# The expert layer's weighted sum on 64x64 quarters of the TensorE array, two gathered rows at a time

## The chip, the cores and the metric

The kernel runs on one core of a Trainium2 chip. The metric is the device time of one execution in microseconds (us), lower is better. A core has five engines with an instruction queue each: TensorE (PE, matmuls, its weight loads shown apart as PEld), VectorE (DVE), ScalarE (ACT), GpSimd (POOL) and SyncE (SP), and 16 DMA engines that move data. Engines wait for each other by semaphores.

## The reference

Two transformer blocks on 512 tokens of width 1024, in float32. The part that matters here is the expert layer of the first block. Each token picks, in each of 8 heads, its 16 best of 16384 experts, so 128 experts a token; an expert is a row u (1024 numbers) and a row v (1024 numbers) of a table. The output is the sum of the v rows, each weighted by gelu(u . x) times its gate:

```python
def one_block(xb):                                   # 128 tokens
    ...
    top_s, pos = lax.top_k(cand_s, PEER_TOPK)
    experts = jnp.take_along_axis(cand_i, pos, axis=-1).reshape(PEER_BLOCK, PEER_HEADS * PEER_TOPK)
    gates = jax.nn.softmax(top_s, axis=-1).reshape(PEER_BLOCK, PEER_HEADS * PEER_TOPK)
    u = u_table[experts]
    hid = jax.nn.gelu(jnp.einsum('nkd,nd->nk', u, xb).astype(jnp.float32), approximate=False) * gates
    return jnp.einsum('nk,nkd->nd', hid.astype(xb.dtype), v_table[experts])
```

## The kernel before

`build` runs the stages one after the other. The one that changes is `peer_experts`. It works on 4 tiles of 128 tokens (`TT`), one token on each of the 128 partitions. A tile has 128 **slots**: slot n is the n-th chosen expert of every token. The slots of one head, 16 of them, are called a **unit** here; there are 32 units. The device loop `Fori(0, PAIRS)` does two units in each round.

What happens to a slot, in order:

1. POOL (L1209) issues one indirect DMA that gathers, for each of the 128 tokens, one row of 8 KB (u and v side by side) into one of the 8 buffers of `rows` (`RING` = 8). Ahead of it POOL waits for `slot_free`, which says that the buffer's former slot has been summed, and once a unit for `routed`, the experts' numbers.
2. DVE (L1286) waits for the landing and forms the dot product of u with the token (`hid`, semaphore `dotted`).
3. ACT takes the gelu (L1330), the product with the gate (L1331), and then writes `diag` (L1333): the 128x128 identity with each row scaled by the token's weight.
4. PE (L1359) waits for `diag_ready` and multiplies `diag` by the v half of the buffer, in two matmuls of 512 columns, which add into `peer_y` in PSUM. Each float32 matmul runs as two passes over the array, so the trace has four MATMUL records a slot. The last one raises `slot_free`.

Between two units DVE does `route`: a long chain of small instructions that finds the 16 experts and gates of the next unit. It begins with a wait for `gates_free`, which ACT raises when it has done all 16 slots of the unit before, and the dots of the next unit stand behind it in DVE's queue. POOL's gathers run up to 8 slots ahead of PE, so the routes are made one unit ahead of the dots: the route of unit u+1 stands ahead of the dots of unit u.

`zero` (L1346) opens and closes each tile's sum with matmuls of zeros. `add_tile` (L1292) adds a tile's sum to `t.x` on DVE; for tile 0 it stands at the end of the loop of tile 1, and so on; those of tiles 2 and 3 both stand at the very end. The order on each engine is the order in which the code is written; there is no scheduler.

Two other lines serve as a comparison. `first_attention` has matmuls with only 64 rows of the array (L571 and L572): two of its products, `score0` and `score1`, use the rows 0 to 63 and 64 to 127. In `scores` they are written as all of half 0, then all of half 1:

```python
for half in range(2):
    rows = slice(half * AHD, (half + 1) * AHD)
    q = t.fm[rows, h, NM + i * P:NM + (i + 1) * P]
    pe.matmul(score[half][:, BANK - NM:BANK], q, t.fm[rows, AH + h, 0:NM], start=True, stop=True)
    pe.matmul(score[half][:, BANK:BANK + (i + 1) * P], q, t.fm[rows, AH + h, NM:NM + (i + 1) * P], ...)
```

Of the kernel before, what the change touches and what calls it, by code (L numbers as in the profile page):

```python
# [18 lines left out]
ALU = mybir.AluOpType  # L19
ACT = mybir.ActivationFunctionType  # L20
AX = mybir.AxisListType

P = 128
D = 1024
KC = D // P
T = 512
TT = T // P
# [3 lines left out]
BANK = 512  # L31
# [10 lines left out]
SLOTS = PH * TOPK  # L42
# [70 lines left out]
def sbuf(nc, ctx, name, shape, dtype=F32):  # L113
    return ctx.enter_context(nc.sbuf_tensor(numbered(name), shape, dtype))


def psum(nc, ctx, name, shape):
    return ctx.enter_context(nc.psum_tensor(numbered(name), shape, F32))
# [1035 lines left out]
def peer_experts(core, t, dram, hidden, scores):  # L1154
# [3 lines left out]
    nc = core.nc  # L1158
    RING, PAIRS = 8, PH // 2
    PER = 2 * TOPK  # L1160
    with ExitStack() as ctx:
        rows = sbuf(nc, ctx, "rows", [P, RING, 2 * D])
        hid = sbuf(nc, ctx, "hid", [P, 3, RING])
        diag = sbuf(nc, ctx, "diag", [P, RING, P])
        zeros = sbuf(nc, ctx, "zeros", [P, BANK])
        step16 = sbuf(nc, ctx, "step16", [P, TOPK])

# [13 lines left out]
        experts = sbuf(nc, ctx, "experts", [P, 2, TOPK], U32)  # L1181
        gates = sbuf(nc, ctx, "gates", [P, 2, TOPK])
        soft = sbuf(nc, ctx, "soft", [P, 3, TOPK])
        y = [psum(nc, ctx, f"peer_y{i}", [P, D]) for i in range(2)]
        step_in, ready, go = core.sem("step16_in"), core.sem("zeros_ready"), core.sem("gather_go")
        got = [core.sem(f"rows_in{i}") for i in range(RING)]
        routed, logits, exped, gates_free = [core.sem(f"peer_{n}") for n in ("routed", "logits", "exped", "gates_free")]
        dotted, diag_ready, slot_free, summed, added = [
            core.sem(f"peer_{n}") for n in ("dotted", "diag_ready", "slot_free", "summed", "added")]
        search_go = core.sem("search_go")  # L1190
        block = ctx.enter_context(nc.Block())

# [21 lines left out]
        def _(dve):  # L1214
            chain = core.chain(dve, "dve_step")
            dve.memset(zeros[:, :], 0.0).then_inc(ready, 1)
            dve.wait_ge(step_in, 16)
            start = chain.count
            per_route = ROUTE_LINKS
# [69 lines left out]

            def add_tile(tile):  # L1290
                dve.wait_ge(summed, tile + 1)
                dve.tensor_tensor(t.x[:, tile, :], t.x[:, tile, :], y[tile % 2][:, :], ALU.add).then_inc(added, 1)  # L1292

            route(0, 0)
            assert chain.count - start == per_route, (chain.count - start)
# [12 lines left out]
        @block.scalar  # L1308
        def _(act):
            chain = core.chain(act, "act_step")  # L1310

            act.sem_inc(gates_free, 1)

            def exponentials(unit):
                act.wait_ge(logits, unit + 1)
                act.activation(soft[:, 1, :], soft[:, 0, :], ACT.Exp).then_inc(exped, 1)

            exponentials(0)
            for tile in range(TT):
                with act.Fori(0, PAIRS) as j:  # L1320
                    chain.base = j * (2 * PER)
                    for p in range(2):

                        act.sem_inc(gates_free, 1)
                        exponentials(tile * PH + j * 2 + (p + 1))
                        for k in range(TOPK):
                            n = p * TOPK + k
                            b = n % RING
                            act.wait_ge(dotted, tile * SLOTS + j * PER + (n + 1))
                            chain.link(act.activation(hid[:, 1, b:b + 1], hid[:, 0, b:b + 1], ACT.Gelu))  # L1330
                            chain.link(act.activation(hid[:, 2, b:b + 1], hid[:, 1, b:b + 1], ACT.Copy,  # L1331
                                                      scale=gates[:, p, k:k + 1]))
                            act.activation(diag[:, b, :], t.ident[:, :], ACT.Copy, scale=hid[:, 2, b:b + 1])\  # L1333
                               .then_inc(diag_ready, 1)
                chain.base = 0
                chain.count += (PAIRS - 1) * 2 * PER

        @block.tensor
        def _(pe):
            pe.sem_inc(slot_free, RING)  # L1340
            pe.wait_ge(ready, 1)

            def zero(tile, start):

                for c in range(2):
                    last = pe.matmul(y[tile % 2][:, c * BANK:(c + 1) * BANK], t.ident[:, :], zeros[:, :],  # L1346
                                     start=start, stop=not start)
                return last

            for tile in range(TT):  # L1350
                if tile >= 2:
                    pe.wait_ge(added, tile - 1)
                zero(tile, True)
                with pe.Fori(0, PAIRS) as j:
                    for n in range(PER):
                        b = n % RING
                        pe.wait_ge(diag_ready, tile * SLOTS + j * PER + (n + 1))
                        for c in range(2):
                            last = pe.matmul(y[tile % 2][:, c * BANK:(c + 1) * BANK], diag[:, b, :],  # L1359
                                             rows[:, b, D + c * BANK:D + (c + 1) * BANK], start=False, stop=False)  # L1360
                        last.then_inc(slot_free, 1)
                zero(tile, False).then_inc(summed, 1)


# [1053 lines left out]
```

## Time and profile before

| | |
|---|---|
| time, median of 3 runs | 3526.93 us (3525.37 to 3530.85) |
| time of the profiled execution | 3526.79 us |
| its span | 3524.7 us |
| expert layer, first gather issued to last sum added | 700.6 to 2126.9 us of the span |
| busy in the span: PE, DVE, ACT, POOL | 78%, 52%, 32%, 19% |

The span is the time from the first to the last instruction in the profile; the execution's own time is 2.1 us longer. The rows below come from several views. The page has the busy share of each engine in 40 equal slices, the granted clock of TensorE (PEclk) and the DMA engines' share and rate. A table of stretches gives the same for stretches of our choice. The timeline has the instructions in order of time, equal neighbours merged, with the idle time of the engine before each in square brackets and who ended it. Busy shares tell how much an engine works; what a stage is bound by is read from who waits for whom.

### The profile page before, as it was taken

To read this page: it belongs to the slowest core of one execution; us is meant where nothing else is said; L and a number is where in the kernel's file an instruction comes from. 1 tells how busy PE (TensorE), PEld (TensorE's weight loads), DVE (VectorE), ACT (ScalarE), POOL (GpSimd) and SP (SyncE) were. 2 spreads that over 40 slices of the span, in tenths; PEclk is the share of its full clock that TensorE was granted. 3 is DMA by queue.
4 is the path that set the end of the run, shared out by engine and by line. 5 is a ranking of instruction groups with operands and counts; after the bars stand their busy time and mean duration, and the time that the engine had idled before them with its cause. 6 is when DMAs were issued, how large, how long until landed. Compare 5 with 4: busy or idle time off the path is not lost. (4 is left out here: it accounts for less than half of the span.)

```text
span 3524.7 us, 32413 instructions
## 1 busy us (share of the span) xinstructions
PE 2754.6 (78%) x10010; PEld 1784.0 (51%) x10010; DVE 1817.2 (52%) x3668; ACT 1123.1 (32%) x2491; POOL 671.8 (19%) x590
## 2 busy tenths in 40 slices
PE   5887778877677767767777676999889786979997
PEld 5864655622223222222232224887778434768875
DVE  5655743366666666666666664332363636243323
ACT  2212322233333333333333333222124235122211
POOL 1100000054444444444444440000000010000000
PEclk8995689988888888988888887999999688989998
DMA  5840012199999999999999992222132000222222
GB/s 181 295 155 1 1 48 78 45 400 381 377 382 377 379 368 381 382 376 381 380 376 379 374 377 94 96 96 72 60 97 62 1 33 1 96 80 100 84 84 78
DMA packets 118429, 705.60 MB, mean 200 GB/s; under 512 B 15184, under 2 KB 15840, under 8 KB 52128
## 3 DMA queue, kind: packets, MB, share of 16 engines
q0 software_dynamic: 81152, 576.40, 41.0%
q1 hardware_dynamic: 37168, 127.76, 10.5%
q8 instruction: 67, 1.10, 0.1%
q14 instruction: 42, 0.34, 0.0%
HBM read 702.01 MB, written 2.10 MB: 200 GB/s over the span
## 5 line engine op out<-in xcount | busy, mean ns | idle before, releaser
L1359 PE MATMUL peer_y<-rows,diag 128*128 128x512 f32 x2048 | 1001.5, 642 | 421.8 <-ACT diag L1333 421.2
L1359 PEld LDWEIGHTS peer_y<-rows,diag 128*128 128x128 f32 x2048 | 404.1, 205 | 1019.2 <-ACT diag L1333 599.7
L1286 DVE CUSTOM_DVE_ANT_0 rows<-rows,hidden 128x1024 f32<-128x1024 f32 x512 | 611.1, 1226 | 435.4 <-DMA rows<-in_peer_table,experts 429.5
L1209 POOL DMA_INDIRECT rows<-in_peer_table,experts x512 | 618.3, 1208 | 914.8 <-PE peer_y L1359 661.0
L1330 ACT ACTIVATE hid<-hid 128x1 f32<-128x1 f32 x512 | 103.9, 203 | 647.3 <-DVE hid L1286 647.2
L1333 ACT ACTIVATE diag<-ident,hid 128x128 f32<-128x128 f32 x512 | 205.5, 401 | 16.8
L1417 DVE TENSOR_TENSOR down_w_low<-down_raw,down_w_high 128x1024 fp32r<-128x1024 f32 x60 | 73.5, 1226 | 254.2 <-ACT down_w_high L1397 254.1
L399 ACT ACTIVATE proj_w_high<-proj_raw 128x1024 fp32r<-128x1024 f32 (+2 forms) x73 | 74.7, 1024 | 323.4 <-PE proj_bank L135 307.6
L426 DVE TENSOR_TENSOR proj_w_low<-proj_raw,proj_w_high 128x1024 fp32r<-128x1024 f32 (+2 forms) x73 | 85.9, 1178 | 147.4 <-ACT proj_w_high L399 145.7
L133 PE MATMUL g_bank<-ffn_feat_high,ffn_w_high 128*128 128x512 f32 x352 | 139.5, 396 | 27.7 <-DVE ffn_w_low L1504 27.7
L1504 DVE TENSOR_TENSOR ffn_w_low<-ffn_raw,ffn_w_high 128x2048 fp32r<-128x2048 f32 x44 | 100.9, 2292 | 115.1 <-ACT ffn_w_high L1486 115.1
L1331 ACT ACTIVATE hid<-hid,gates 128x1 f32<-128x1 f32 x512 | 150.9, 295 | 16.6
L133 PE MATMUL down_bank<-down_w_high,act_t_high 128*128 128x512 f32 x352 | 139.0, 395 | 16.5 <-DVE down_w_low L1417 16.5
L1512 DVE TENSOR_TENSOR silu<-silu,u_bank 128x512 f32<-128x512 f32 x44 | 30.3, 688 | 231.5 <-PE u_bank L135 231.5
L1397 ACT ACTIVATE down_w_high<-down_raw 128x1024 fp32r<-128x1024 f32 x60 | 63.6, 1060 | 262.6 <-PE down_bank L135 247.4
L134 PE MATMUL g_bank<-ffn_feat_low,ffn_w_high 128*128 128x512 f32 x352 | 138.8, 394 | 0.0
L135 PE MATMUL g_bank<-ffn_feat_high,ffn_w_low 128*128 128x512 f32 x352 | 138.7, 394 | 0.0
L134 PE MATMUL down_bank<-down_w_low,act_t_high 128*128 128x512 f32 x352 | 138.5, 393 | 0.0
L135 PE MATMUL down_bank<-down_w_high,act_t_low 128*128 128x512 f32 x352 | 138.3, 393 | 0.0
L133 PE MATMUL u_bank<-ffn_feat_high,ffn_w_high 128*128 128x512 f32 x352 | 137.0, 389 | 0.0
L135 PE MATMUL u_bank<-ffn_feat_high,ffn_w_low 128*128 128x512 f32 x352 | 137.0, 389 | 0.0
L134 PE MATMUL u_bank<-ffn_feat_low,ffn_w_high 128*128 128x512 f32 x352 | 137.0, 389 | 0.0
(420 smaller groups left out, 4558.5 us busy)
## 6 DMA issues: line engine op xcount, KB each, us to landing
ada<-in_w_ada POOLq DMA_DIRECT2D x48, 768.0 KB, 4.8
ffn_raw<-in_ffn_w_gate SPq DMA_DIRECT2D x44, 512.0 KB, 3.6
ffn_raw<-in_ffn_w_up SPq DMA_DIRECT2D x44, 512.0 KB, 4.5
down_raw<-in_ffn_w_down SPq DMA_DIRECT2D x44, 512.0 KB, 3.4
proj_raw<-in_w_in_f SPq DMA_DIRECT2D x16, 512.0 KB, 5.3
proj_raw<-in_peer_w_query SPq DMA_DIRECT2D x16, 512.0 KB, 3.3
rows<-in_peer_table,experts POOLq DMA_INDIRECT x512, 11.9
down_raw<-in_w_out SPq DMA_DIRECT2D x16, 512.0 KB, 3.5
```

Of the source, the lines that this page charges most:

```text
L133: pe.matmul(out, left[0], right[0], start=start, stop=False)
L134: pe.matmul(out, left[0], right[1], start=False, stop=False)
L135: return pe.matmul(out, left[1], right[0], start=False, stop=stop)
L399: act.activation(w.high[:, n % RING, 0:taken(slab)], w_raw[:, n % RAW, 0:taken(slab)], ACT.Copy)\
L426: dve.tensor_tensor(w.low[:, n % RING, 0:taken(slab)], w_raw[:, n % RAW, 0:taken(slab)], w.high[:, n % RING, 0:taken(slab)].bitcast(F32), ...
L1209: pool.indirect_dma_start(rows[:, n % RING, :], None, dram["peer_table"], bass.IndirectOffsetOnAxis(ap=experts[:, p, k:k + 1], axis=0))\
L1286: dve.tensor_tensor_reduce(out=rows[:, b, 0:D], in0=rows[:, b, 0:D], in1=hidden[:, tile, :], scale=1.0, scalar=0.0, op0=ALU.mult, op1=ALU.add,
L1330: chain.link(act.activation(hid[:, 1, b:b + 1], hid[:, 0, b:b + 1], ACT.Gelu))
L1331: chain.link(act.activation(hid[:, 2, b:b + 1], hid[:, 1, b:b + 1], ACT.Copy, scale=gates[:, p, k:k + 1]))
L1333: act.activation(diag[:, b, :], t.ident[:, :], ACT.Copy, scale=hid[:, 2, b:b + 1])\
L1359: last = pe.matmul(y[tile % 2][:, c * BANK:(c + 1) * BANK], diag[:, b, :], rows[:, b, D + c * BANK:D + (c + 1) * BANK], start=False, stop= ...
L1504: dve.tensor_tensor(w.low[:, f % 2, :, :], w_raw[:, f % 2, :, :], w.high[:, f % 2, :, :].bitcast(F32), ALU.subtract).then_inc(low.handle, 1)
```

## The change

A diagonal matrix has only zeros outside its diagonal blocks, so of the 128x128 array three quarters of a pass multiply nothing but the diagonal. The change keeps only two 64x64 blocks of each `diag`: block g holds the tokens of half g (partitions 0 to 63 or 64 to 127), and both stand side by side in a `diag` of 128x64. The array is used as four 64x64 quarters. A quarter is given by its rows (which half of the tokens comes in, g) and its columns (which half of the PSUM partitions goes out). Slot s of a pair uses the columns of half s. So even slots sum into partitions 0 to 63 and odd slots into 64 to 127, and each token half g has banks of its own: `peer_y00`, `peer_y01` for even tiles, `peer_y10`, `peer_y11` for odd ones (the last digit is g).

What this brings with it:

- PE waits for two diagonals, then issues 8 matmuls for two slots (before 2 for each slot), in the order (g, s) = (0,0), (1,1), (0,1), (1,0), for either 512 columns, and frees both buffers at the last one.
- ACT writes `diag` from `folded` (128x64) rather than from the identity (128x128). `folded` is made once by two copies on DVE.
- `zero` has 8 matmuls of 64x512 rather than 2 of 128x512.
- Half of each tile's sum lies on the other half's partitions. ACT's `cross` copies those two pieces into `crossed` at the end of a tile's loop, and `add_tile` now has two adds of 64x1024 from PSUM, and, once `cross_done` is there, one of 128x1024 with `crossed`.

```diff
-        diag = sbuf(nc, ctx, "diag", [P, RING, P])
+        folded = sbuf(nc, ctx, "folded", [P, HALVES])
+        diag = sbuf(nc, ctx, "diag", [P, RING, HALVES])
...
+            for own in GROUPS:
+                last = dve.tensor_copy(folded[own, :], t.ident[own, own])
+            last.then_inc(fold_done, 1)
...
             def add_tile(tile):
                 dve.wait_ge(summed, tile + 1)
-                dve.tensor_tensor(t.x[:, tile, :], t.x[:, tile, :], y[tile % 2][:, :], ALU.add).then_inc(added, 1)
+                for g, own in enumerate(GROUPS):
+                    last = dve.tensor_tensor(t.x[own, tile, :], t.x[own, tile, :], y[tile % 2][g][own, :], ALU.add)
+                last.then_inc(added, 1)
+                dve.wait_ge(added, 2 * tile + 1)
+                dve.wait_ge(cross_done, tile + 1)
+                dve.tensor_tensor(t.x[:, tile, :], t.x[:, tile, :], crossed[:, :], ALU.add).then_inc(added, 1)
...
+            def cross(tile):
+
+                act.wait_ge(summed, tile + 1)
+                if tile:
+                    act.wait_ge(added, 2 * tile)
+                for g, own in enumerate(GROUPS):
+                    last = act.activation(crossed[own, :], y[tile % 2][g][GROUPS[1 - g], :], ACT.Copy)
+                last.then_inc(cross_done, 1)
...
-                            act.activation(diag[:, b, :], t.ident[:, :], ACT.Copy, scale=hid[:, 2, b:b + 1])\
+                            act.activation(diag[:, b, :], folded[:, :], ACT.Copy, scale=hid[:, 2, b:b + 1])\
                                .then_inc(diag_ready, 1)
                 chain.base = 0
                 chain.count += (PAIRS - 1) * 2 * PER
+                if tile >= 1:
+                    cross(tile - 1)
+            cross(TT - 1)
...
-                    for n in range(PER):
-                        b = n % RING
-                        pe.wait_ge(diag_ready, tile * SLOTS + j * PER + (n + 1))
+                    for n in range(0, PER, 2):
+                        pe.wait_ge(diag_ready, tile * SLOTS + j * PER + (n + 2))
+                        pe.sem_inc(slot_go, 1)
                         for c in range(2):
-                            last = pe.matmul(y[tile % 2][:, c * BANK:(c + 1) * BANK], diag[:, b, :],
-                                             rows[:, b, D + c * BANK:D + (c + 1) * BANK], start=False, stop=False)
-                        last.then_inc(slot_free, 1)
+                            for g, s in ((0, 0), (1, 1), (0, 1), (1, 0)):
+                                b, rows_of = (n + s) % RING, GROUPS[g]
+                                last = pe.matmul(y[tile % 2][g][GROUPS[s], c * BANK:(c + 1) * BANK],
+                                                 diag[rows_of, b, :], rows[rows_of, b, D + c * BANK:D + (c + 1) * BANK],
+                                                 start=False, stop=False)
+                        last.then_inc(slot_free, 2)
```

How this stands in the engines' queues. First PE at the start of a tile's loop. Before, with a wait ahead of each slot's two matmuls:

```order
L1359 MATMUL peer_y0<-rows,diag 128x512 [waits peer_diag_ready]
L1359 MATMUL peer_y0<-rows,diag 128x512
L1357 REGISTER_ALU
L1359 MATMUL peer_y0<-rows,diag 128x512 [waits peer_diag_ready]
L1359 MATMUL peer_y0<-rows,diag 128x512
L1357 REGISTER_ALU
```

And in the changed kernel (`peer_y00` takes what comes in from tokens 0 to 63, `peer_y01` what comes from 64 to 127):

```order
L1390 MATMUL peer_y00<-rows,diag 64x512 [waits peer_diag_ready]
L1390 MATMUL peer_y01<-rows,diag 64x512
L1390 MATMUL peer_y00<-rows,diag 64x512
L1390 MATMUL peer_y01<-rows,diag 64x512
L1390 MATMUL peer_y00<-rows,diag 64x512
L1390 MATMUL peer_y01<-rows,diag 64x512
L1390 MATMUL peer_y00<-rows,diag 64x512
L1390 MATMUL peer_y01<-rows,diag 64x512
L1385 REGISTER_ALU
```

Eight matmuls now stand behind one wait where two stood, and neighbours alternate between the two row halves.

Second DVE at the very end of the layer, where the sums of tiles 2 and 3 are added. Before this is one row for both, and in the changed kernel:

```order
L1302 TENSOR_TENSOR x<-x,peer_y 64x1024 [waits peer_summed]
L1302 TENSOR_TENSOR x<-x,peer_y 64x1024
L1306 TENSOR_TENSOR x<-x,crossed 128x1024 [waits cross_done,peer_added]
L1302 TENSOR_TENSOR x<-x,peer_y 64x1024 [waits peer_summed]
L1302 TENSOR_TENSOR x<-x,peer_y 64x1024
L1306 TENSOR_TENSOR x<-x,crossed 128x1024 [waits cross_done,peer_added]
```

Each add became three, the third of which waits for ACT as well.

## Rows read from the trace of the kernel before

**Rows 1.** The page: busy share of the DMA engines, in tenths, in 40 slices.

```profile
DMA  5840012199999999999999992222132000222222
```

**Rows 2.** Table of stretches: length, busy us (instructions) of each engine, PEclk, DMA share, GB/s.

```profile
711.00:2128.00 1417.00, 1013.53 (x2076) 409.43 (x2076) 903.65 (x2270) 546.53 (x1629) 610.38 (x504) 0.87 0.93 377
```

**Rows 3.** The same table, one unit from the end of a route on.

```profile
797.00:800.00 3.00, 0.00 (x0) 0.00 (x0) 2.70 (x11) 1.50 (x2) 0.00 (x0) 0.69 1.02 423
...
800.00:806.00 6.00, 1.73 (x2) 0.84 (x3) 5.67 (x13) 2.22 (x8) 0.00 (x0) 0.50 1.01 421
...
808.00:810.00 2.00, 2.00 (x6) 0.93 (x5) 2.00 (x3) 1.64 (x6) 0.94 (x1) 0.91 0.00 0
...
812.00:816.00 4.00, 4.00 (x11) 1.85 (x10) 1.23 (x2) 0.48 (x3) 2.02 (x4) 1.00 1.00 416
816.00:820.00 4.00, 4.00 (x11) 1.74 (x10) 1.24 (x2) 1.59 (x5) 2.92 (x3) 1.00 0.96 348
...
826.00:834.00 8.00, 6.50 (x14) 2.22 (x13) 4.25 (x8) 2.69 (x9) 6.10 (x4) 1.00 1.01 426
```

**Rows 4.** Timeline of POOL: one restart's first two gathers, then first and last restart.

```profile
808.86 0.94 POOL L1209 DMA_INDIRECT rows<-in_peer_table,experts  x1 [14.08 <-PE peer_y L1359]
810.80 1.28 POOL L1209 DMA_INDIRECT rows<-in_peer_table,experts  x1 [1.00 <-PE peer_y L1359]
...
718.46 0.94 POOL L1209 DMA_INDIRECT rows<-in_peer_table,experts  x1 [7.73 <-PE peer_y L1359]
...
2095.43 0.94 POOL L1209 DMA_INDIRECT rows<-in_peer_table,experts  x1 [13.71 <-PE peer_y L1359]
```

**Rows 5.** Timeline of ACT and PE: first two diagonals of that unit, first matmuls.

```profile
803.82 0.40 ACT L1333 ACTIVATE diag<-ident,hid 128x128 f32<-128x128 f32 x1
...
804.27 22.90 PE L1359 MATMUL peer_y<-rows,diag 128*128 128x512 f32 x48 [11.24 <-ACT diag L1333]
...
804.97 0.40 ACT L1333 ACTIVATE diag<-ident,hid 128x128 f32<-128x128 f32 x1
```

**Rows 6.** Timeline of the weight loads; these start with passes 4 to 7.

```profile
806.99 0.34 PEld L1359 LDWEIGHTS peer_y<-rows,diag 128*128 128x128 f32 x1 [0.52 <-ACT diag L1333]
807.85 0.34 PEld L1359 LDWEIGHTS peer_y<-rows,diag 128*128 128x128 f32 x1 [0.52 <-issue]
808.54 0.19 PEld L1359 LDWEIGHTS peer_y<-rows,diag 128*128 128x128 f32 x1 [0.36 <-issue]
808.97 0.19 PEld L1359 LDWEIGHTS peer_y<-rows,diag 128*128 128x128 f32 x1 [0.24 <-issue]
```

**Rows 7.** Timeline of the same unit's second half, dots that wait for the gather.

```profile
830.36 1.23 DVE L1286 CUSTOM_DVE_ANT_0 rows<-rows,hidden 128x1024 f32<-128x1024 f32 x1 [1.26 <-DMA rows<-in_peer_table,experts]
...
832.84 1.22 DVE L1286 CUSTOM_DVE_ANT_0 rows<-rows,hidden 128x1024 f32<-128x1024 f32 x1 [1.24 <-DMA rows<-in_peer_table,experts]
```

**Rows 8.** Attention, 64 rows a pass: the clock, all four passes, then the first two.

```profile
358.00:360.00 2.00, 2.00 (x8) 0.85 (x8) 0.00 (x0) 0.53 (x2) 0.00 (x0) 0.50 0.00 0
...
358.36 2.06 PE L572 MATMUL score<-fm 64*128 64x512 f32 x4
...
358.36 1.21 PE L572 MATMUL score<-fm 64*128 64x512 f32 x2
```

**Rows 9.** Groups by line (xcount | busy us, mean ns | idle us before): ACT.

```profile
L1333 ACT ACTIVATE diag<-ident,hid 128x128 f32<-128x128 f32 x512 | 205.5, 401 | 16.8
L1331 ACT ACTIVATE hid<-hid,gates 128x1 f32<-128x1 f32 x512 | 150.9, 295 | 16.6
...
L1917 ACT ACTIVATE mla_k<-mla_bank 64x512 f32<-64x512 f32 x8 | 4.7, 590 | 12.4 <-PE mla_bank L1983 12.4
```

**Rows 10.** Timeline where tile 0's sum is added, at the end of tile 1.

```profile
1410.98 1.22 DVE L1292 TENSOR_TENSOR x<-x,peer_y 128x1024 f32<-128x1024 f32 x1
...
1412.11 0.29 DVE L1233 COPY s_now<-scores 128x256 f32 x1
```

**Rows 11.** Timeline of the end of the layer.

```profile
2125.70 1.22 DVE L1292 TENSOR_TENSOR x<-x,peer_y 128x1024 f32<-128x1024 f32 x1 [3.65 <-PE peer_y L1346]
```

More of the change, by code:

```diff
@@ L1160, in peer_experts @@
     PER = 2 * TOPK
+    HALVES = P // 2
+    GROUPS = [slice(0, HALVES), slice(HALVES, P)]
     with ExitStack() as ctx:
@@ L1183, in peer_experts @@
         soft = sbuf(nc, ctx, "soft", [P, 3, TOPK])
-        y = [psum(nc, ctx, f"peer_y{i}", [P, D]) for i in range(2)]
+        y = [[psum(nc, ctx, f"peer_y{i}{g}", [P, D]) for g in range(2)] for i in range(2)]
+        crossed = sbuf(nc, ctx, "crossed", [P, D])
         step_in, ready, go = core.sem("step16_in"), core.sem("zeros_ready"), core.sem("gather_go")
@@ L1189, in peer_experts @@
             core.sem(f"peer_{n}") for n in ("dotted", "diag_ready", "slot_free", "summed", "added")]
+        fold_done, cross_done = core.sem("fold_done"), core.sem("cross_done")
+        slot_go = core.sem("slot_go")
         search_go = core.sem("search_go")
@@ L1312, in _ @@
             act.sem_inc(gates_free, 1)
+            act.wait_ge(fold_done, 1)
+            def cross(tile):
[5 more added lines that the diff above has]
+                last.then_inc(cross_done, 1)
             def exponentials(unit):
@@ L1345, in zero @@
                 for c in range(2):
-                    last = pe.matmul(y[tile % 2][:, c * BANK:(c + 1) * BANK], t.ident[:, :], zeros[:, :],
-                                     start=start, stop=not start)
+                    for own in GROUPS:
+                        for g, rows_of in enumerate(GROUPS):
+                            last = pe.matmul(y[tile % 2][g][own, c * BANK:(c + 1) * BANK], t.ident[rows_of, rows_of],
+                                             zeros[rows_of, :], start=start, stop=not start)
                 return last
@@ L1351, in _ @@
                 if tile >= 2:
-                    pe.wait_ge(added, tile - 1)
+                    pe.wait_ge(added, 2 * (tile - 1))
                 zero(tile, True)
                 with pe.Fori(0, PAIRS) as j:
-                    for n in range(PER):
-                        b = n % RING
-                        pe.wait_ge(diag_ready, tile * SLOTS + j * PER + (n + 1))
+                    for n in range(0, PER, 2):
+                        pe.wait_ge(diag_ready, tile * SLOTS + j * PER + (n + 2))
+                        pe.sem_inc(slot_go, 1)
                         for c in range(2):
-                            last = pe.matmul(y[tile % 2][:, c * BANK:(c + 1) * BANK], diag[:, b, :],
-                                             rows[:, b, D + c * BANK:D + (c + 1) * BANK], start=False, stop=False)
-                        last.then_inc(slot_free, 1)
+                            for g, s in ((0, 0), (1, 1), (0, 1), (1, 0)):
[4 more added lines that the diff above has]
+                        last.then_inc(slot_free, 2)
                 zero(tile, False).then_inc(summed, 1)
```

## The prediction

> **What bounds the kernel now.** I read the page first, then a table of stretches, then the timeline of one unit. The page shows the DMA engines at nine tenths or more through the whole expert layer [rows 1]. The stretch of the layer says the same more exactly: 1417 us, DMA share 0.93 at 377 GB/s, PE busy for 1014 us, DVE for 904 us [rows 2]. So the first suspicion is that halving PE's work hides behind the gathers. But 0.93 isn't 1, and the missing part is where the change can act.
>
> Where slots come one by one, DVE's dots wait for the landing and start 2.48 us apart (830.36 and 832.84 [rows 7]). A gather is 128 rows of 8 KB, 1.05 MB, which at 426 GB/s [rows 3] is 2.46 us: here the DMA engines are the limit, and 16 slots are worth 39.7 us. PE needs less: 4 passes of 0.43 us (808.54 to 808.97 [rows 6]), 1.7 us a slot. Yet a unit takes longer. First gathers after a unit's restart are issued at 718.46 and, 31 units on, at 2095.43 [rows 4]: 44.4 us a unit. The other 4.7 us are a hole: the DMA engines move nothing from 808 to 810 [rows 3], and recover slowly after it.
>
> The hole comes from a chain, once a unit: the last dot of a unit, ACT's three steps, `gates_free`, DVE's route, the first dot, its diagonal, PE's first passes, `slot_free`, POOL's next gather. POOL stood idle for 14.08 us before 808.86, until PE let it go [rows 4], and the 8 buffers in flight last less long than the chain. **Each microsecond on that chain makes each unit a microsecond longer.** It passes through PE just where PE is slowest: the clock fell during the route (0.69, then 0.50 [rows 3]) and the unit's first passes run at 0.50, 0.86 us apart (806.99 to 807.85 [rows 6]). So what counts is not PE's throughput but the time from the first finished dot to the first freed buffer.
>
> **The change part by part.** The sum is made against the profiled execution's own 3526.8 us, practically the median.
>
> *The wait for the second diagonal.* The first two diagonals start at 803.82 and 804.97 [rows 5], so PE begins 1.15 us later. Nothing hides it: all 8 buffers are full or being summed, and POOL has nothing else to issue.
>
> *A narrower diagonal.* ACT takes 401 ns for 128 columns and 295 ns for one [rows 9]; for 64 the line between gives about 348. It stands on the chain twice, ahead of the first matmuls and ahead of `gates_free`: 0.10 us less. Together +1.05 us a unit.
>
> *The passes.* Before, the first buffer came free after 4 passes. Now a pair needs 16, of quarter size. How many lie side by side isn't shown for quarters, so it is bounded by the nearest rows. For row halves the attention shows it. At half clock (0.50) a 512-column pass takes 0.86 us, and four one after the other would take over 3.4 us; those of L572 took 2.06 us, and the first two of them lie within 1.21 us [rows 8]. They can't be the two passes of one product. So `score1` began before `score0` was done, though it stands behind it in PE's queue: the row halves run beside each other, each in its own order. For 64 rows a pass isn't shorter.
>
> For the two column halves of one row half no row tells. With both column halves free and each row half kept in order, the first pass of the next matmul starts with the second pass of the one before: a row half's 4 matmuls of a pair (8 passes) take 5 rounds. If all four quarters are free of each other, it is 4 rounds, as before. If the column halves exclude each other, it is 8. I take 5, because the order within a row half is what the attention's rows bear out, and two passes of one matmul use the same quarter. The fifth pass costs 0.69 us (807.85 to 808.54, the clock rises in it [rows 6]). In the steady part a pair then needs 4 rounds of 0.43 = 1.7 us in 4.96 us, so PE never limits there, and freeing buffers in twos leaves some four of the 8 buffers queued for DMA (two wait for their pair, two are summed).
>
> *Per unit:* 1.05 + 0.69 = 1.74 us. The first unit has no hole to widen: its first release comes 18 us after the first gather was issued, and 8 gathers take 19.8. So 31 units: **+53.9 us**.
>
> *Tile ends.* Before, the 1.22 us add of tile 0 begins at 1410.98 beside ACT's last three steps, and the route starts at 1412.11 [rows 10], when ACT too is through. Now ACT, from then on, does two copies of 64x1024 from PSUM. Such a copy of 512 columns takes 0.59 us [rows 9]; for 1024 I take 1.0 us, between that and twice that. Then DVE adds 128x1024, 1.22 us. The route starts at about 1415.4 rather than 1412.1: +3.3 us, on the chain, at the ends of tiles 1 and 2. **+6.6 us.** DVE's two adds of 64x1024 are over by then, beside ACT's copies.
>
> *The layer's end.* Before, one add of 1.22 us follows PE's last zeros at 2125.70 [rows 11]. Now two copies on ACT beside two adds on DVE (2.4 us), then one more add: +2.4 us, and the fifth round +0.4. **+2.8 us.**
>
> *At no cost:* the two small copies that make `folded` (DVE waits for a load there anyway), and `zero`, 16 passes in 4 rounds where 4 passes stood. If quarters didn't overlap, `zero` would cost PE 5 us a tile, still inside the route's wait.
>
> Sum: 3526.8 + 53.9 + 6.6 + 2.8 = 3590.1 us.
>
> **A rule of the Trainium skill against the rows.** The rows of the attention show passes that start ahead of older ones. The Trainium skill, "TensorE: Matmul & The Clock Gate", section "Part 3: Packing small matmuls — row/col tiling", says that matmuls start and end strictly in program order. By that rule a pair's 8 matmuls, alternating as they do, would need 8 rounds, and the sum would be that of the rival below; the trace disagrees for row halves [rows 8]. The same section reports measured gains for packing by columns too (2.38 times for three column tiles), which speaks for 4 or 5 rounds; no row here shows it.
>
> **The rivals.**
>
> *All four quarters free (4 rounds).* Then only the 1.05 us is left: 32.6 + 6.6 + 2.4 = 41.6, 3568 us. For it: nothing in the rows forbids it. Against it: each row half kept its own order.
>
> *Eight rounds.* Column halves exclude each other, or the queue is strictly in order. Four more passes than the first four before the first release: before, that is the time between the first two gathers, 808.86 and 810.80, 1.94 us [rows 4]. 31 x (1.05 + 1.94) = 92.7, + 6.6, + 2.4 and 8 more rounds of 0.43 at the end = 3.4: 3632 us. PE would still keep up (3.4 us in 4.96).
>
> *No overlap at all: the change doesn't do what it says.* 8 passes of 0.43 = 3.44 us a slot, over the 2.48 of the gather. PE would become the bound: 512 x 3.44 = 1761 us, against 32 x 44.4 = 1421 now: +340, with the ends some 3875 us. The attention's rows speak against it.
>
> *Part of the hole is given back.* After the restart the rate stays at 416 and 348 GB/s from 812 to 820 where 426 is normal [rows 3]: (4 x 10 + 4 x 78) / 426 = 0.83 us of transfer a unit. If buffers freed in twos fill that dip, 26 us come off: 3564 with 5 rounds, 3543 with 4. But gathers follow each other by 1.94 us before [rows 4], less than the 2.48 that one takes, so the queue isn't short in the dip.
>
> *The other side: the clock doesn't fall.* If the first pair ran at 0.43 us a pass instead of 0.86, its 5 rounds would release the buffers 2.1 us sooner, so a unit would be 0.4 us shorter than before, and 1.74 - 2.1 = -0.4, x 31 = -12, + 9.4: 3524 us; with 4 rounds (-0.85 a unit) 3510 us. It decides once the granted clock stays near 1.0 through the route. Now it falls to 0.50 by 800 while PE is idle (0.00 us busy from 797 to 800 [rows 3]), and the change leaves PE idle there for at least as long.
>
> **How the numbers follow.** Five rounds 0.40; four rounds 0.24; eight rounds 0.18; no overlap 0.04; a part given back 0.06; the clock stays up 0.08, half of it faster, half of it about the same. Forecast: 3590 us. The range must reach to four and to eight rounds, with some us for the copies on ACT (0.6 to 1.2 us each instead of 1.0): 3560 to 3640 holds about 0.85. A change of 0.2% (7 us) is about what a measurement of this kernel can tell from none: faster 0.04, within 0.04, slower 0.92.
>
> **What the changed kernel's profile would show.** From the start of a unit's first diagonal to the first new gather it takes 5.04 us before (803.82 [rows 5] to 808.86 [rows 4]); then 6.8, with four rounds 6.1, with eight 8.1. The time without DMA traffic in each unit grows by the same. Restarts of units stand 46.2 us apart instead of 44.4. The first pair's 16 passes lie in 5 rounds of 0.86 us at a clock of 0.50. PE's busy time in the layer falls to about half without a gain. At the ends of tiles 1 and 2 the route starts some 3.3 us later. What would make it wrong: restarts at 44.4 us, which would say that the hole isn't on the path; or a clock near 1.0 at the first pair. The other stages stay as they are.

## The result and the profile after

The changed kernel takes 3555.1 us (median of 4 runs, 3547.6 to 3559.37) against 3527.05 us before: a ratio of 1.0077, with a 95% interval of 1.0059 to 1.0094. It is slower, as forecast, but by 28 us rather than 63, and outside the range by 5 us. Its profiled execution took 3559.4 us, 32.6 us more than the profiled one of before, so the two traces differ by somewhat more than the medians.

First the stretch of the expert layer in the table of stretches (columns as in [rows 2], which it answers to), then the page's clock and DMA rows (the second answers to [rows 1]).

```profile
715.00:2162.00 1447.00, 698.21 (x4208) 203.50 (x4208) 913.62 (x2279) 527.07 (x1637) 561.74 (x504) 0.71 0.90 369
```

```profile
PEclk8995689966776766677777777999989699989998
DMA  5840012199999999899989993222222000212222
```

PE is busy for 698 us instead of 1014, the granted clock fell from 0.87 to 0.71, and the DMA share from 0.93 to 0.90. PE got much less to do and the layer got longer. (What the quarters leave out is the two blocks off the diagonal, half of the array, and not three quarters of a pass as the section on the change says.)

A unit's first new gather is called its **restart** from here on. The restart of one unit in the timeline of the changed kernel. These rows answer to [rows 4, 5]:

```profile
811.03 0.35 ACT L1357 ACTIVATE diag<-folded,hid 128x64 f32<-128x64 f32 x1
...
811.52 9.97 PE L1390 MATMUL peer_y<-rows,diag 64*64 64x512 f32 x64 [10.91 <-ACT diag L1357]
...
816.04 0.94 POOL L1215 DMA_INDIRECT rows<-in_peer_table,experts  x1 [12.40 <-PE peer_y L1390]
817.29 0.94 POOL L1215 DMA_INDIRECT rows<-in_peer_table,experts  x1 [0.30 <-issue]
```

The diagonal that PE waits for is now the unit's second (811.03; the first began at 809.88), and from the first diagonal to the first new gather it takes 816.04 - 809.88 = 6.16 us instead of 5.04. PE's first matmul begins 0.14 us after that second diagonal's end (811.03 + 0.35 to 811.52); before it was 0.05 us (804.22 to 804.27 [rows 5]). How many rounds the 16 passes take is seen in the timeline of the weight loads, which start in step with the passes and answer to [rows 6]:

```profile
811.49 0.34 PEld L1390 LDWEIGHTS peer_y<-rows,diag 64*64 64x64 f32 x8 [12.36 <-issue]
812.40 0.28 PEld L1390 LDWEIGHTS peer_y<-rows,diag 64*64 64x64 f32 x4 [0.57 <-issue]
813.25 0.28 PEld L1390 LDWEIGHTS peer_y<-rows,diag 64*64 64x64 f32 x4 [0.57 <-issue]
814.10 0.28 PEld L1390 LDWEIGHTS peer_y<-rows,diag 64*64 64x64 f32 x4 [0.57 <-issue]
```

They come in fours, 0.85 us apart at half clock (0.50), the first eight being the four quarters' first pass and the one loaded ahead. **All four quarters run side by side: 4 rounds, not 5.** The first passes of the four quarters start within 20 ns, so the third and fourth matmul are under way before the first one's second pass. The prediction quoted a rule of strict program order from the Trainium skill ("TensorE: Matmul & The Clock Gate", section "Part 3: Packing small matmuls — row/col tiling") and made 8 rounds of it. Counted by passes, the trace disagrees with that rule, for column halves too; counted by whole matmuls, 4 rounds keep it, as each of the eight can then start and end no earlier than the one before (the records don't say which pass is whose), and the 8 rounds didn't follow from it. What the same section says of the gain by packing rows and columns agrees in its direction: 16 passes took the time of 4.

Where the time is. The layer is split here at its first gather, the units' restarts, the last dot and the end of the last add, all read from the two timelines:

| us | before | after | difference |
|---|---|---|---|
| first gather to first new gather | 17.8 | 18.9 | +1.1 |
| first to last restart (31 units) | 1377.0 | 1402.2 | +25.3 |
| of it: last dot of tiles 1 and 2 to the next dot | 26.7 | 32.8 | +6.1 |
| last restart to last dot | 24.3 | 24.2 | 0.0 |
| last dot to the end of the last add | 7.2 | 11.2 | +4.0 |
| layer | 1426.3 | 1456.6 | +30.3 |

A unit takes 45.2 us instead of 44.4. Without the two tile ends that is 19.2 / 31 = 0.62 us a unit. The prediction had 1.74.

What makes up the 0.62 us is read from the DMA packets of the trace. For each of the 30 inner units I counted the bytes moved from 3 to 14 us after its restart, and took what is missing to 424 GB/s, the full rate, in microseconds of transfer. Before it is 0.96 us a unit; after, 0.37. So the wait costs 1.08 us (6.12 against 5.04 from first diagonal to first new gather, means of the 30 units), the last dot to the next dot 0.08 more, and 0.59 us is given back after the restart: +0.57.

The stretch from 7 to 11 us after a restart shows it, here that of the ninth unit. Before:

```profile
1081.10:1085.10 4.00, 4.00 (x11) 1.78 (x10) 1.25 (x4) 1.78 (x6) 3.22 (x3) 1.00 0.97 317
```

and in the changed kernel:

```profile
1093.20:1097.20 4.00, 0.27 (x4) 0.30 (x8) 1.45 (x5) 1.69 (x6) 2.84 (x3) 0.58 1.00 422
```

The rate is 422 GB/s instead of 317, while the DMA share says nearly the same (1.00 and 0.97). The packets themselves were slow before, not few (the share counts the time that packets are under way).

### The profile page after: what moved, and what is told of

Read it like the earlier page. It is cut to its first block and busy times, and to the rows that moved or that the text cites. A ratio compares the mean times of both kernels' runs of the same rounds, so it can differ in the third digit from the quotient of the medians.

```text
span 3557.2 us, 36727 instructions
## 1 busy us (share of the span) xinstructions
PE 2434.6 (68%) x12154; PEld 1576.6 (44%) x12154; DVE 1829.0 (51%) x3678; ACT 1103.2 (31%) x2499; POOL 623.6 (18%) x590
## 5 line engine op out<-in xcount | busy, mean ns | idle before, releaser
L1390 PE MATMUL peer_y<-rows,diag 64*64 64x512 f32 x4096 | 686.2, 817 | 764.6 <-ACT diag L1357 764.5
L1390 PEld LDWEIGHTS peer_y<-rows,diag 64*64 64x64 f32 x4096 | 198.6, 174 | 1250.7 <-issue 1250.7
L1215 POOL DMA_INDIRECT rows<-in_peer_table,experts x512 | 569.7, 1113 | 988.1 <-PE peer_y L1390 740.1
L1357 ACT ACTIVATE diag<-folded,hid 128x64 f32<-128x64 f32 x512 | 178.0, 348 | 16.8
L1544 DVE TENSOR_TENSOR silu<-silu,u_bank 128x512 f32<-128x512 f32 x44 | 30.3, 688 | 231.3 <-PE u_bank L135 231.3
```

Source lines behind the costliest of these rows:

```text
L1215: pool.indirect_dma_start(rows[:, n % RING, :], None, dram["peer_table"], bass.IndirectOffsetOnAxis(ap=experts[:, p, k:k + 1], axis=0))\
L1357: act.activation(diag[:, b, :], folded[:, :], ACT.Copy, scale=hid[:, 2, b:b + 1])\
L1390: last = pe.matmul(y[tile % 2][g][GROUPS[s], c * BANK:(c + 1) * BANK], diag[rows_of, b, :], rows[rows_of, b, D + c * BANK:D + (c + 1) * BANK],
```

## Experiments

The theory: a unit is as long as the chain through PE's first passes makes it, so only the time to the first freed buffer counts. The rivals: the hole isn't on the path; or the quarters or the crossing cost the time. The table gives for all runs, from their profiles, the means over the 30 inner units, worked out as above: time per unit over the 31 restarts (tile ends in it), first diagonal to first new gather, and what is missing to the full rate from 3 to 14 us after a restart. after_again is the changed kernel once more.

| kernel | time us | ratio (95%) | layer us | us a unit | diagonal to gather | missing |
|---|---|---|---|---|---|---|
| before | 3527 to 3528 | 1 | 1426.3 | 44.42 | 5.04 | 0.96 |
| the change | 3555.1 | 1.0077 (1.0059 to 1.0094) | 1456.6 | 45.23 | 6.12 | 0.37 |
| after_again | 3556.1 | 1.0076 (1.0058 to 1.0094) | 1452.3 | 45.15 | 6.11 | 0.35 |
| pair_wait_only | 3580.7 | 1.0145 (1.0123 to 1.0167) | 1481.1 | 46.07 | 6.21 | 1.06 |
| pair_free_in_twos | 3628.9 | 1.0280 (1.0256 to 1.0305) | 1529.2 | 47.57 | 8.75 | 0.41 |
| quarters_by_slot | 3518.9 | 0.9978 (0.9966 to 0.9991) | 1418.9 | 44.10 | 4.93 | 0.28 |
| one_column_half | 3536.8 | 1.0023 (1.0013 to 1.0032) | 1435.5 | 44.64 | 4.98 | 0.98 |
| wait_for_four | 3641.7 | 1.0321 (1.0298 to 1.0344) | 1547.9 | 48.07 | 8.47 | 0.93 |
| no_crossing (one run) | 3518.5 | | 1413.6 | 43.97 | 4.95 | 0.24 |
| quarters_by_columns | 3482.7 | 0.9868 (0.9846 to 0.9890) | 1383.9 | 43.03 | 3.33 | 0.47 |

The layer's first gather was issued between 699.9 and 709.5 us in these profiles, though next to nothing ahead of it differs; the layer's own time is the better measure of a few us.

Every kernel here but the one before also has `pe.sem_inc(slot_go, 1)` behind PE's wait, a semaphore that nobody waits for. In all of them PE's first matmul of a unit begins 0.14 us after the end of the diagonal that it waits for, and in the kernel before 0.05 us. So 0.09 us a unit (3 us in all) most likely belong to this instruction; no run leaves it out alone.

**pair_wait_only.**

```diff
-                    for n in range(PER):
-                        b = n % RING
-                        pe.wait_ge(diag_ready, tile * SLOTS + j * PER + (n + 1))
+                    for n in range(0, PER, 2):
+                        pe.wait_ge(diag_ready, tile * SLOTS + j * PER + (n + 2))
+                        pe.sem_inc(slot_go, 1)
+                        for s in range(2):
+                            b = (n + s) % RING
...
-                        last.then_inc(slot_free, 1)
+                            last.then_inc(slot_free, 1)
```

> The kernel before with one part of the change alone: PE waits for two diagonals, then does the 128x128 passes of both slots and frees each buffer after its own four passes. Theory (the chain through PE's first passes sets the length of a unit): the first release of each unit comes 1.15 us later, nothing else changes, 31 x 1.15 = +36 us, 3563 us, and the first diagonal to first new gather takes 6.2 us instead of 5.04. Rival (the hole without DMA traffic isn't on the path): 3527 us.

Measured: +54 us. The hole is on the path, and the first new gather comes 1.17 us later, as the chain has it. But a unit is 1.65 us longer, not 1.15. The timeline at a restart of this kernel shows the rest:

```profile
814.56 1.22 DVE L1286 CUSTOM_DVE_ANT_0 rows<-rows,hidden 128x1024 f32<-128x1024 f32 x1
814.61 1.98 POOL L1209 DMA_INDIRECT rows<-in_peer_table,experts  x1 [13.53 <-PE peer_y L1361]
```

The gather begins just after that dot has begun and takes 1.98 us. In the kernel before it begins at 808.86 [rows 4], 0.01 us ahead of the next dot, and takes 0.94; in the changed kernel 0.04 us ahead of one. That dot of the kernel before:

```profile
808.87 1.25 DVE L1286 CUSTOM_DVE_ANT_0 rows<-rows,hidden 128x1024 f32<-128x1024 f32 x1
```

This is no accident of one place. Over all 512 gathers of the kernel before, the 307 that begin outside a dot, or in its last 0.1 us, take 0.94 us in the mean, and so do 8 that begin in a dot's first 0.04 us. The other 197 begin inside one and end 0.81 to 0.84 us after that dot's end (in this kernel 176, 0.82 in the mean). **A gather that begins inside a running dot waits for that dot's end.** The reverse isn't so: where a dot begins while such a free gather runs (108 times before), the dot takes 1.23 us and the gather 0.94, as good as alone. The Trainium skill, "SBUF — State Buffer", section "Terms", says that the two engines arbitrate for one pair of ports, held by one of them for its full instruction. The trace agrees with it for a gather begun inside a dot, and doesn't for a dot begun inside a gather; that it is these ports that the gather waits for, no run here shows. In 21 of the 30 units here the first packets of the new gather came 2.7 us after its begin instead of 1.65, in the mean 2.38. That accounts for the rest: 1.17 us of the chain and 0.72 of later packets, less 0.27, since behind its first packets this kernel's slow stretch is the milder one (0.69 us missing against 0.96, counted from the first packets on; the 1.06 of the table holds the late start too), is 1.62 us.

**pair_free_in_twos.**

```diff
                         for s in range(2):
...
-                            last.then_inc(slot_free, 1)
+                        last.then_inc(slot_free, 2)
```

> As the kernel with the pair's wait alone, but both buffers are freed together after all eight full passes. Chain: 1.15 + 1.94 = 3.09 us a unit, +96 us, 3623 us, if the slow stretch 7 to 11 us after a restart comes from PE's full passes (then it stays). If that slow stretch comes from gathers that are issued one by one with a short queue, it goes, 0.7 us a unit less: 3601 us.

Measured: +102 us. The total lies near the first case and yet the slow stretch went, from 1.06 us missing to 0.41, with full passes on PE. The first two microseconds of the ninth unit's stretch:

```profile
1120.70:1122.70 2.00, 2.00 (x6) 0.76 (x4) 0.01 (x1) 0.83 (x3) 1.70 (x2) 1.00 0.98 397
```

So full passes by themselves aren't its cause. The price of the eight passes was too low: the diagonal to the new gather takes 8.75 us, 2.54 more than with the pair's wait alone, where I had read 1.94 off one unit [rows 4]; the mean of the first two gathers' distance before is 2.3 us. By these means a unit should be 3.15 us longer (3.72 on the chain, less 0.55 given back), and it is.

**quarters_by_slot.**

```diff
-                    for n in range(0, PER, 2):
-                        pe.wait_ge(diag_ready, tile * SLOTS + j * PER + (n + 2))
+                    for n in range(PER):
+                        pe.wait_ge(diag_ready, tile * SLOTS + j * PER + (n + 1))
...
+                        b, s = n % RING, n % 2
                         for c in range(2):
-                            for g, s in ((0, 0), (1, 1), (0, 1), (1, 0)):
-                                b, rows_of = (n + s) % RING, GROUPS[g]
+                            for g, rows_of in enumerate(GROUPS):
...
-                        last.then_inc(slot_free, 2)
+                        last.then_inc(slot_free, 1)
```

> The changed kernel with the pairing undone: quarters of 64x64, but each slot waits for its own diagonal and frees its own buffer (even slots on one column half, odd slots on the other). Theory: the wait for the second diagonal is what cost the time. Then the first release comes 0.1 to 0.2 us sooner than in the kernel before, and what stays is the crossing at the tiles' ends (+9 us): 3531 us, or 3509 if the slow stretch after a restart goes as well, as it did in the changed kernel. Rival (the quarters themselves are slow, or the crossing costs more than 9 us): 3550 us or more.

Measured: 3518.9 us, 36 us less than the change, 0.2% less than before. With the pair's wait undone the quarters cost nothing. Neighbouring slots use different column halves and so overlap, several of the new gathers follow each other by 1.3 us where PE had paced all of them at 1.7 to 1.8, and the slow stretch is gone.

**one_column_half.**

```diff
-                        b, s = n % RING, n % 2
+                        b, s = n % RING, 0
```

> As quarters_by_slot, but every slot uses the same column half, so slots follow each other on PE at the old pace of 1.7 us while each pass still uses only 64x64 quarters. It separates two causes of the slow stretch 7 to 11 us after a restart. If it comes from gathers that are issued at PE's pace of about 1.8 us rather than 1.3 us, it comes back: 0.28 us lost a unit there becomes about 1.0, 3519 + 0.7 x 31 = 3541 us. If it came from the full 128x128 passes, it stays away: 3519 us.

Measured: 3536.8 us, and the missing 0.98 us are back, exactly as before, with the passes still of 64x64. The ninth unit's stretch again:

```profile
1088.50:1092.50 4.00, 4.00 (x20) 1.35 (x18) 1.23 (x2) 1.14 (x5) 2.12 (x3) 1.00 0.97 346
```

So the slow stretch goes with how the buffers are freed after a restart: 0.96, 1.06, 0.98 and 0.93 us are missing where PE frees one buffer every 1.7 to 1.8 us, 0.24 to 0.47 where they are freed in twos or at the dots' pace. Another thing goes with it: in those four kernels PE is busy through all of the 4 us, in the others for 2.5 us at most. PE's work alone doesn't do it, though. Two stretches of the kernel before:

```profile
1081.10:1083.10 2.00, 2.00 (x6) 0.95 (x5) 0.23 (x3) 0.90 (x3) 1.70 (x2) 1.00 0.95 283
...
1085.10:1089.10 4.00, 4.00 (x11) 1.84 (x10) 1.83 (x3) 0.92 (x4) 2.69 (x3) 1.00 1.00 418
```

PE is just as busy from 11 to 15 us after the restart, at 418 GB/s; and from 7 to 9 us it is busy throughout in pair_free_in_twos as well, which moves 397 GB/s there against 283 (397 against 338 in the mean of the units). Why the packets get slow when buffers come free one by one, no run here tells.

**no_crossing.** The crossing's copies and the third add are left out of quarters_by_slot, so that half of each slot's sum is missing.

```diff
-                dve.wait_ge(cross_done, tile + 1)
-                dve.tensor_tensor(t.x[:, tile, :], t.x[:, tile, :], crossed[:, :], ALU.add).then_inc(added, 1)
+                dve.sem_inc(added, 1)
...
-                for g, own in enumerate(GROUPS):
-                    last = act.activation(crossed[own, :], y[tile % 2][g][GROUPS[1 - g], :], ACT.Copy)
-                last.then_inc(cross_done, 1)
+                act.sem_inc(cross_done, 1)
```

> quarters_by_slot without the crossing: ACT's copies and DVE's third add are left out, so the half of each slot's sum that lies on the other partitions is missing. From the last dot of a tile to the next dot 13.3 us instead of 16.4 at the ends of tiles 1 and 2, and 2.3 us less at the layer's end; everything else the same, 8 to 9 us less, about 3510 us in this one look. If the boundary's cost lies elsewhere, 16.4 stays.

Measured: at the ends of tiles 1 and 2, 14.9 and 15.1 us from dot to dot, not 13.3; with the crossing it is 16.4. At the layer's end 8.5 us instead of 9.7. So less than half of the tile end's 3.1 us is the crossing. The rest is mostly that two adds of 64 partitions take twice as long as one of 128 (2.45 us for 1.22), as the timeline of the changed kernel shows at the end of tile 1 (it answers to [rows 10]):

```profile
1424.93 2.45 DVE L1302 TENSOR_TENSOR x<-x,peer_y 64x1024 f32<-64x1024 f32 x2
...
1425.99 2.05 ACT L1335 ACTIVATE crossed<-peer_y 64x1024 f32<-64x1024 f32 x2
...
1428.14 1.23 DVE L1306 TENSOR_TENSOR x<-x,crossed 128x1024 f32<-128x1024 f32 x1 [0.76 <-ACT crossed L1335]
1429.28 0.29 DVE L1242 COPY s_now<-scores 128x256 f32 x1
```

(The end of tile 0, where nothing is added, is 0.35 us longer as well than before, in every kernel with quarters; no run says why.) The layer's time fell by 5.3 us; the execution's didn't, as its layer began 4.4 us later.

**wait_for_four.** pair_wait_only with fours in place of twos (`range(0, PER, 4)`, a wait for `n + 4`, `s` from 0 to 3).

> The kernel before, but PE waits for four diagonals, then sums and frees slot by slot. It tests the chain's price and why the pair's wait alone cost 1.65 us a unit rather than 1.15. Chain alone: 3 x 1.15 = 3.45 us a unit, 107 us, 3634 us. If the 0.5 us over came from the first new gather meeting a running dot of DVE (as in 22 of 30 units there, where it took 1.98 us instead of 0.94 and its first packets came 2.7 us after it instead of 1.65), it is gone here, since the dots are over by then: 3634 us, first packets 1.65 us after the gather. If any late gather is slow, 3650 us.

Measured: +114 us, 3.65 us a unit. The gather comes 3.43 us later, as forecast (3.45), and its packets 1.83 us after it in the mean, between the two cases: part of the units' first gathers still meet a dot, since the next dot may begin just then. In its total the chain's price holds up to three times the change's wait, but it isn't all one hole: the rate falls once more in the middle of a unit, to 226 to 361 GB/s from 23 to 27 us after a restart, and the hole at the restart is shorter in return. That the second dip comes from four buffers that wait for each other is likely, and no run shows it by itself.

**quarters_by_columns**, a version of my own. The column halves of the array take the two 512-column halves of v rather than two slots:

```diff
-                    for n in range(0, PER, 2):
-                        pe.wait_ge(diag_ready, tile * SLOTS + j * PER + (n + 2))
-                        pe.sem_inc(slot_go, 1)
-                        for c in range(2):
-                            for g, s in ((0, 0), (1, 1), (0, 1), (1, 0)):
-                                b, rows_of = (n + s) % RING, GROUPS[g]
-                                last = pe.matmul(y[tile % 2][g][GROUPS[s], c * BANK:(c + 1) * BANK],
-                                                 diag[rows_of, b, :], rows[rows_of, b, D + c * BANK:D + (c + 1) * BANK],
-                                                 start=False, stop=False)
-                        last.then_inc(slot_free, 2)
+                    for n in range(PER):
+                        pe.wait_ge(diag_ready, tile * SLOTS + j * PER + (n + 1))
+                        pe.sem_inc(slot_go, 1)
+                        b = n % RING
+                        for g, c in ((0, 0), (1, 1), (0, 1), (1, 0)):
+                            rows_of = GROUPS[g]
+                            last = pe.matmul(y[tile % 2][g][GROUPS[c], :], diag[rows_of, b, :],
+                                             rows[rows_of, b, D + c * BANK:D + (c + 1) * BANK],
+                                             start=False, stop=False)
+                        last.then_inc(slot_free, 1)
```

`y` is one bank for each g, `crossed` 512 columns wide, and `add_tile` has four adds of 64x512.

> A version of my own: the column halves of the array hold the two 512-column halves of one slot rather than two slots, so that a slot takes 2 rounds of four quarters instead of 4 passes, waits for its own diagonal and frees its own buffer. The crossing is half as wide. Theory (latency to the first release counts): 1.71 us sooner through the rounds at half clock and 0.1 to 0.2 through the narrower diagonal, 1.9 x 31 = -58 us, +7 at the tiles' ends: 3476 us, 3454 if the slow stretch goes too; where the hole closes altogether, less is gained. Rival (PE's part isn't on the path): 3527 to 3535 us.

Measured: 3482.7 us, 1.3% less than the kernel before. A slot needs 2 rounds, and the gather follows the first diagonal by 3.33 us instead of 5.04. Its timeline at a restart:

```profile
805.08 0.35 ACT L1361 ACTIVATE diag<-folded,hid 128x64 f32<-128x64 f32 x1
...
805.57 7.00 PE L1393 MATMUL peer_y<-rows,diag 64*64 64x512 f32 x39 [11.29 <-ACT diag L1361]
...
808.55 1.32 POOL L1215 DMA_INDIRECT rows<-in_peer_table,experts  x1 [12.49 <-PE peer_y L1393]
```

The 1.70 us of the chain came, yet a unit is only 1.39 us shorter. The slow stretch gave another 0.68 (0.28 us missing against 0.96, counted from the first packets on). Against it stand the gather, which now meets a running dot (it takes 1.32 us above), so that its first packets come 2.16 us after it rather than 1.66: 0.50 us; and the tile ends, 5.0 us in all: 0.16 us a unit. That leaves 1.7, 0.3 more than measured. The rest is likely that there is little hole left to close: in the mean of the units the rate is under 45 GB/s for three microseconds before, from 1 us ahead of the new gather on, and for one here. From here on a shorter chain brings less.

## Why the prediction was wrong, point by point

- **What bounds the kernel**: right. A chain once a unit, through PE's first passes at half clock, leaves the DMA engines idle. pair_wait_only, wait_for_four and quarters_by_columns lengthen and shorten it, and the time follows. That PE's throughput doesn't matter is shown by the change itself (698 us busy instead of 1014, and slower) and by one_column_half.
- **The second diagonal's wait, 1.15 less 0.10 for the narrower diagonal**: right in size on the chain ahead of the gather, +1.08, in part by luck. Its parts in the mean of the units are 1.15 for the wait, 0.05 less for the narrower diagonal, 0.09 more between the diagonal and the first matmul (the added `sem_inc`, most likely, for which I had counted nothing) and 0.10 less from there to the gather. The second 0.05, ahead of `gates_free`, didn't come: the last dot to the next dot went from 13.03 to 13.11 us outside the tile ends. The first unit did pay as well, +1.1 us, where I had counted nothing.
- **The passes: the step that failed.** I took 5 rounds, +0.69 us a unit, from the order that the attention's rows keep within a row half. It was 4 rounds, which was the first rival (from the first matmul to the restart 4.49 us in the mean, 4.58 before). That is 31 x 0.69 = 21 us of the 35 too many. The attention's products used the full column width, so the order seen within a row half was also the order within one part of the array, and said nothing of two column halves; I read more into it than it shows. The rule of program order, which I took as worth 8 rounds, would have given 4 if applied to whole matmuls.
- **The part given back: the second step that failed.** I held the dip from 812 to 820 [rows 3] for independent of how the buffers are freed, since gathers 1.94 us apart outrun transfers of 2.48. It wasn't: 0.59 us a unit, 18 us. That rival's price was right (0.83 us at most), its chance (0.06) and the argument against it were not. The two failed steps together, rivals with 0.24 and 0.06, gave 3543 us in the prediction, and the range, laid to reach four and eight rounds one at a time, held no room for both at once. The 12 us from there to 3555 are mostly that 0.59 us a unit came back and not 0.83 (7 us) and that the waits came to 1.16 and not 1.05 (3 us).
- **The tile ends**: 3.2 and 2.9 us measured, 3.3 forecast, for partly the wrong reason. I had DVE's half adds beside ACT's copies at no cost; without the copies the tile ends still cost 1.7 us (1.23 by the second half add, 0.35 as at the end of tile 0).
- **The layer's end**: 4.0 us, 2.8 forecast. PE's last pair ran at a clock of 0.50 and took 3.37 us; before, the last slots' passes ran at 1.00. In the run after_again the stretch from the last dot to the end took 9.8 us instead of 11.2. The rows stand below.
- **The clock that stays up**: didn't happen. The first pair ran at 0.50, as before, and the rest of the layer got slower clocks too (0.71 in the mean). PE's busy time therefore fell to 69% and not to half, as the prediction's signs had it. The sum of this rival for four rounds was off too: 1.05 less four passes of 0.43 is -0.67 us a unit, not -0.85, and 3515 us rather than 3510.

The end of the layer in the table of stretches and the timeline of the changed kernel:

```profile
2150.00:2154.00 4.00, 1.81 (x12) 0.61 (x12) 3.67 (x4) 2.50 (x5) 0.00 (x0) 0.50 0.00 0
...
2152.45 3.37 PE L1390 MATMUL peer_y<-rows,diag 64*64 64x512 f32 x16 [2.19 <-ACT diag L1357]
```

and the same stretch of the kernel before:

```profile
2119.00:2124.00 5.00, 4.03 (x10) 1.74 (x10) 2.37 (x3) 1.33 (x5) 0.00 (x0) 1.00 0.00 0
```

With the measured terms the sum is 31 x (1.08 + 0.08 - 0.59) = 17.7, the tile ends 6.1, the first unit 1.1, the end 4.0: 28.9 us, of 30.3 in the layer.

## What to carry to other kernels

Where a stage waits once a round on a chain of several engines, price a change by what it does to the time until the first buffer is freed, not by how much of an engine's work it saves; grouping two items behind one wait puts the second item's latency on that chain. If an array can be split in four, give the parts to one item, so that it is done sooner (quarters_by_columns, -44 us), rather than to two items that must wait for each other (the change, +28 us). And where two rivals on one side are both cheap to imagine, the range has to hold their sum.

## What the runs showed of the hardware

- Four 64x64 quarters of the array run float32 passes fully side by side: their first passes start 7 ns apart, and a quarter starts its first pass ahead of the second pass of an older matmul on another quarter. A quarter's pass takes as long as a full one, 0.85 us at half clock and 0.43 at full.
- A gather issued by GpSimd inside a running VectorE dot ends 0.8 us after the dot, though alone it takes 0.94; a dot begun while a gather runs isn't held up (1.23 us). A chain can so gain or lose 1 us by 0.05 us of alignment.
- After a pause, 8 KB gather packets are slower for some 4 us when PE frees the buffers one by one, 1.7 to 1.8 us apart, and not when they are freed in twos or faster, though either is faster than the 2.48 us that one gather takes. In the kernel before, a packet begun 7 us after a restart took 0.41 us in the mean, in the changed one 0.33, and 0.31 is normal. The cause stays open.
- VectorE's add of 64 partitions by 1024 takes 1.22 us, as long as that of 128 partitions.
- With PE at 48% busy instead of 72% in the layer, the granted clock was 0.71 instead of 0.87 of full speed.
